# The first block's weights in four units of two feature tiles instead of two of four

## The reference

```python
def rms_norm(x, g):
    xf = x.astype(jnp.float32)
    y = xf * lax.rsqrt(jnp.mean(xf * xf, axis=-1, keepdims=True) + RMS_EPS)
    return (y * g.astype(jnp.float32)).astype(x.dtype)

def nsa_gmlp_mixer(h, w_in, ...):
    proj = jnp.einsum("bsd,de->bse", h, w_in)
    ...
    q, k_c, v_c, k_s, v_s, k_w, v_w, gate_logits, u, v = jnp.split(proj, points, axis=-1)
    kc = compress_tokens(heads_kv(k_c), cmp_pos_k, cmp_w1_k, cmp_w2_k)
```

## Time and profile before

| | |
|---|---|
| median of three runs | 973.7 us (973.39 to 975.74) |
| the profiled execution's own time | 973.98 us |
| its span, first to last instruction | 972.0 us |
| TensorE busy | 97% of the span |
| VectorE, ScalarE, GpSimd busy | 69%, 56%, 25% |
| what ended last, by engine | PE 80%, DVE 8%, ACT 6%, DMA 3% |

### The profile page before, as it was taken

The page is one execution under the profiler, slowest core; times in us unless marked ns, Lnnn a source line. Parts: engine busy times, 40 slices in busy tenths (PEclk is TensorE's granted clock), DMA queues, the critical chain, the costliest instruction groups (busy, mean ns, idle before and its releaser), DMA issues.

```text
span 972.0 us, 16471 instructions
## 1 busy us (share of the span) xinstructions
PE 946.3 (97%) x6121; PEld 829.3 (85%) x6121; DVE 669.4 (69%) x1094; ACT 544.4 (56%) x956; POOL 242.2 (25%) x239
## 2 busy tenths in 40 slices
PE   9999999999999999999999999999999999999997
PEld 8987777888877798899989999998889778888786
DVE  5765567777785668975668666677985767755453
ACT  6667666444443666834547455557863754544443
POOL 5205002111122231299932143330230021000100
PEclk9999999999999999999999999999999999999999
DMA  9755347789987713760139756653246677656561
GB/s 293 217 161 190 94 147 231 229 276 289 284 274 257 247 51 97 208 174 22 34 102 311 236 165 183 172 144 88 75 147 213 219 237 242 211 175 192 194 221 66
DMA packets 141594, 179.04 MB, mean 184 GB/s; under 512 B 8124, under 2 KB 117390, under 8 KB 141520
## 3 DMA queue, kind: packets, MB, share of 16 engines
q1 hardware_dynamic: 130624, 144.53, 47.6%
q0 software_dynamic: 10304, 33.18, 11.5%
q10 hardware_dynamic: 592, 0.34, 0.1%
HBM read 176.90 MB, written 1.12 MB: 183 GB/s over the span
## 4 chain that ended last, share of the span: by engine, by line
PE 80%; DVE 8%; ACT 6%; DMA 3%; issue 2%; SPq 0%; DVEq 0%; ACTq 0%
PE bank L1932 26%; PE bank L2021 12%; PE bank L2023 11%; PE bank L2022 11%; DVE w_lo L1333 3%; ACT w_hi L869 2%; PE bank L2191 1%; PE bank L2454 1%; PE bank L1963 1%; PE bank L2450 1%; PE bank L2477 1%; DMA w_raw<-in_w_in 1%; PE bank L2385 1%; PE bank L2073 1%; DMA w_raw<-in_w_down 1%
## 5 line engine op out<-in xcount | busy, mean ns | idle before, releaser
L1333 DVE TENSOR_TENSOR w_lo<-w_raw,w_hi 128x1024 fp32r<-128x1024 f32 (+1 forms) x239 | 286.0, 1221 | 91.2 <-ACT w_hi L869 86.8
L869 ACT ACTIVATE w_hi<-w_raw 128x1024 fp32r<-128x1024 f32 (+1 forms) x258 | 262.1, 1037 | 117.7 <-PE bank L2023 50.6
L1932 PE MATMUL bank<-h_hi,w_hi 128*128 128x256 f32 x560 | 162.9, 291 | 1.9 <-DVE w_lo L1333 1.0
L1932 PE MATMUL bank<-h_lo,w_hi 128*128 128x256 f32 x560 | 158.3, 283 | 0.0
L1932 PE MATMUL bank<-h_hi,w_lo 128*128 128x256 f32 x560 | 158.2, 282 | 0.0
L2021 PE MATMUL bank<-w_hi,h_hi 128*128 128x512 f32 x384 | 152.1, 396 | 1.9 <-DVE h_lo L1333 1.9
L2023 PE MATMUL bank<-w_hi,h_lo 128*128 128x512 f32 x384 | 150.3, 391 | 0.0
L2022 PE MATMUL bank<-w_lo,h_hi 128*128 128x512 f32 x384 | 150.1, 391 | 0.0
L1932 PEld LDWEIGHTS bank<-h_hi,w_hi 128*128 128x128 f32 x560 | 107.2, 191 | 3.4 <-DVE w_lo L1333 2.0
L1932 PEld LDWEIGHTS bank<-h_lo,w_hi 128*128 128x128 f32 x560 | 107.3, 192 | 0.0
L1932 PEld LDWEIGHTS bank<-h_hi,w_lo 128*128 128x128 f32 x560 | 107.1, 191 | 0.0
(11 more groups left out here) (463 smaller groups left out, 1810.3 us busy)
## 6 DMA issues: line engine op xcount, KB each, us to landing
w_raw<-in_w_in SPq DMA_DIRECT2D x84, 512.0 KB, 3.8
ada_raw<-in_ada_w POOLq DMA_DIRECT2D x48, 512.0 KB, 6.0
w_raw<-in_w_gate_up SPq DMA_DIRECT2D x88, 256.0 KB, 5.4
w_raw<-in_w_ffn_in SPq DMA_DIRECT2D x88, 256.0 KB, 4.0
w_raw<-in_w_down SPq DMA_DIRECT2D x22, 512.0 KB, 6.5
w_raw<-in_w_ffn_out SPq DMA_DIRECT2D x22, 512.0 KB, 4.5
w_raw<-in_w_out SPq DMA_DIRECT2D x16, 512.0 KB, 4.0
w_raw<-in_w_o_ssd SPq DMA_DIRECT2D x16, 512.0 KB, 3.4
```

What stands on the lines that cost most here:

```text
L869: act.activation(high(u, n), w_raw[:, u % RING, 0:n], ACT.Copy).then_inc(hi_ready, 1)
L1333: return dve.tensor_tensor(dst, src, hi.bitcast(F32), ALU.subtract)
L1932: ins = pe.matmul(out_b[:, s, :], w[:, kk, c], x[:, k0 + k, :], start=k == 0 and s == 0 and step == 0, stop=k == sum(st.ks) - 1 and s == 1 ...
```

## The change

The first stream's block is cut into four units of two tiles. Each has its own load (256 KB), high part and low part. Ahead of each pair of h, ScalarE and VectorE now split one unit. All other streams keep their units.

```diff
-    s_kc = Stream(1, (4, 4), "dve")
+    s_kc = Stream(1, (2, 2, 2, 2), "dve")
     s_gv = Stream(2, (4, 4), "act")
...
             act.activation(st4[:, t, 8:9], st4[:, t, 5:6], ACT.Sqrt, bias=eps, scale=1.0 / D).then_inc(x_sd, 1)
-        split_to(1)
         for p in range(4):
-            if p == 2:
-                split_to(2)
+            split_to(p + 1)
             act.wait_ge(hT_ready, p + 1)
...
         rstd_x(0, 1)
-        split_to(1)
         for p in range(4):
-            if p == 2:
-                split_to(2)
+            split_to(p + 1)
             dve.wait_ge(h_hi_ready, p + 1)
```

## The result

| | before | changed |
|---|---|---|
| median | 973.44 us | 977.76 us (8 runs) |
| ratio, with its 95% interval | | 1.0042 (1.0032 to 1.0051) |
| the profiled execution's own time | 973.98 us | 978.39 us |
| its span | 972.0 us | 976.7 us |

What follows compares the result with a forecast made beforehand. TensorE, busy 97% of the span, was taken as the bound, so only its start could pay: -0.33 us there, +0.33 given back at 24.5, total 0.0, hence 974.0, taken as 973.9 us; range 972.6 to 976.3.

Steps and rivals of the forecast that it cites:

- What bounds the start: First block: h becomes the bound, TensorE starts at 11.37 in place of 11.70, a gain of 0.33 us.
- Running through: First block's 48 products: VectorE (1.36 us a pair) and ScalarE (1.27) stay hidden under TensorE (1.50).
- What the ring does: Four-slot weight ring: small units fill it, so token-unit loads wait, leaving near 9.1, 11.9, 13.3 and 14.7 us.
- I take 4.2, between 3.5 and 4.5: L = 16.1: Second token unit's load, issued at 11.9, takes 4.2 us and lands at 16.1, leaving nothing of the 0.33 gain.
- the upper bound: Second token unit's load could take 6.6 us, like one issued at 10.9 behind others, landing at 18.5: +2.4 us.
- the lower bound: Second token unit's load could take 3.5 us, as this shape of load alone did, landing at 15.4: -0.33 us.
- The estimate of 3.2 us: Second token unit's load by the skill's cost table: 3.2 us, landing at 15.1, so the 0.33 gain is kept.
- T + 6.33: Second token block starts 6.33 us after the small copies start at T, unless TensorE's first token block ends later (24.46).
- L + 2.37: Small copies start 2.37 us after the second token unit lands at L, or at 18.02 if that is later.
- Rival (b): Second token unit lands at 16.5 to 18.5, TensorE waits before the second token block: +0.4 to +2.4 us; chance 0.16.
- rival (c): Second token unit's load takes 7.1 us or more, landing from 19.0 on: slower by over 2.9 us; chance 0.04.
- passed on and not multiplied: After 24.8 us: the shift at the second token block carries through later loads without growing; 1 us allowed either way.

Runs made afterwards that it cites:

- rows behind the bias loads: GpSimd's two layer-norm row loads issued after the bias loads: in the changed kernel 974.16 us (1.0004), in the kernel before 975.88 us (1.0025).
- rows between: GpSimd's two row loads held until the second token unit's high part: changed kernel 972.75 us (0.9999), kernel before 972.53 us (0.9993).
- TensorE kept busy: Changed kernel with 24 unused products between the first and second token block, in TensorE's wait: 976.31 us (1.0029).
- copies first: Changed kernel with VectorE's low part of the second token unit moved behind the small copies: 975.76 us (1.0023).
- the second pair held: Kernel before with the second token unit's load held until the second pair of h has its low part: 976.80 us (1.0037).
- held, third pair: Kernel before with the second token unit's load held until the third pair of h has its low part: 978.09 us (1.0058).
- changed once more: The changed kernel itself, unaltered, timed again with a second profile: 977.16 us (1.0046).
- halves in the slots: Kernel before, first units cut into halves within their slots, token loads issued without a wait: 972.79 us (0.9989); with rows held as well, 973.03 us (0.9998).

## Why the prediction was wrong

- **What bounds the start**: right. h became the bound, first product at 11.37 in the trace, 11.37 predicted, a gain of 0.33.
- **Running through**: right. No wait within the 48 products (5.99 us in the traces); the small low parts took 0.68 to 0.69.
- **What the ring does**: right in every issue. The four loads of the token units left at 9.0, 11.9, 13.3 and 14.7 (9.1, 11.9, 13.3 and 14.7 predicted).
- **"I take 4.2, between 3.5 and 4.5: L = 16.1"**: this step failed. The load took 6.83 us, L = 18.73; in five more traces with the rows beside it, issued at 11.9 to 12.5, it took 6.1 to 6.9. I took the weight queue's share from 12 to 18 us of before (0.20 MB a microsecond) as what it gets beside GpSimd's rows. In that stretch it had been fed since the start; in the changed kernel its load came after the rows, and it got 0.18 MB in 4 us. I had named the upper bound, 6.6 us for the load at 10.9, and set it aside because that one "had another large load ahead of it". Both were at work there. With the rows moved, the same load of the kernel before, issued at 11.1 (rows behind the bias loads) and at 11.4 (rows between), lands after 5.3 us in place of 6.6: the rows made 1.3 us of it, and the other 1.8 over the 3.5 of a load alone remain without them. In the changed kernel the load ahead is nearly through (it lands at 13.3), but the rows alone are enough: without them the same issue lands after 3.6 us (3.7 with the rows between), close to the lower bound. That 6.83 came so near the upper bound of 6.6 is a coincidence, since rows and load ahead had different shares in the two. The estimate of 3.2 us that the prediction takes from the Trainium skill, "DMA: Bandwidth & Descriptors", is under the 3.6; that table stands there for loads that GpSimd issues, and this one is SyncE's.
- **T + 6.33**: right. With L = 18.73 it gives 27.43; the trace has 27.37, so +2.6 from the kernel before. The two parts are each off by some 0.1 us and cancel: T is L + 2.25 and not L + 2.37, and TensorE goes at T + 6.39. Rival (b) had this mechanism, and its end, +2.4, was nearly the truth; it got 0.16.
- **A term that was missing**: the sum and all rivals had TensorE's wait at its own length. The wait was followed by a fall of the clock worth 1.5 us in the profile (7.47 less 5.98), and the medians agree: +2.6 with TensorE kept busy, +4.2 to +4.3 without. The late load by itself, +2.6 over the measured 973.44, would have ended at 976.0, inside the range; the clock took the result past 976.3 and past the 2.9 us that rival (c) needed.
- **"passed on and not multiplied"**: right up to the k and v block (+3.9 there). The trace ends 4.7 later; of the rest, 0.3 comes between 70 and 90 us and 0.5 between 303 and 308, and neither is shown to belong to the change.

Open: how often the clock falls in that block. Two profiles of the changed kernel, with equal waits, show it once; the mean clocks show only that falls are more frequent in the changed kernel (6 of 13 executions at 0.996 or less, none of 89 before), not where they lie. Nor do they follow the length of this one wait alone: with the copies first, where TensorE waits 1.5 us, it is 4 of 12, and with the second pair held, 2.3 us, 1 of 5.

## What to carry to other kernels

Cutting a unit in a ring also takes slots: ask which later load now stands behind the ring's wait, when it will leave, and what runs on the DMA engines at that moment. A share of bandwidth read from a stretch in which a queue was full in advance was no guide here to what a load got that arrived second. And when a change can open a gap on the engine that sets the pace, price the gap with and without a fall of its clock behind it.

## What was not expected of the hardware

- With two loads on it that spread a row over 128 partitions, 256 KB each, GpSimd's queue held 75.2% of the DMA engines' time for 0.63 MB from 12 to 16 us, and the weight queue moved 0.18 MB; with them away, it was 0.13 MB in 8.5% and 0.83 MB in 78.7%. From 13 to 15 us the weight queue got 0.01 MB, though two to three units of 512 KB were waiting in it. The Trainium skill, "DMA: Bandwidth & Descriptors", in the rules for kernel authors, says that all issuing engines' transfers share the same 16 DMA engines and interleave. The traces agree that they share; the shares were far from even.
- The fall of the granted clock to half cost 1.5 us in a block of 48 products of 256 columns and came in some executions only: in the profiles it began between 28 and 30 us (changed; held, third pair), between 48 and 50 (both kernels with the rows behind the bias loads), between 104 and 106 (changed once more; held, second pair), between 124 and 132 (before; changed, a second fall; both with halves in the slots), and in five profiles nowhere ahead of the last microseconds. The lowest time of a profiled execution, 970.47 us (changed, rows between), had none. In the kernel before, the 33 executions with a mean clock of 0.999 or more took 972.7 us on average, the other 56 973.8.
